# T5 bias of a hybrid decoder layer: read with a positive step from shifted rows instead of reversed on TensorE, and one evacuation of x ahead of a weight split

## The reference, cut to what matters

```
mod = silu(c) @ w_ada + b_ada -> shift1, scale1, gate1, shift2, scale2, gate2
h = rms_norm(x) * (1 + scale1) + shift1                # x is 1024 tokens x 1024
q, k, v, xs, z, B, C, dt = split(h @ w_in)             # one combined projection
a = softmax(q k^T / 8 + bias[head, distance], sinks) v # window 128, 8 heads, blocks of 128
s = Mamba-2 SSD(conv(xs, B, C), dt, A), gated by silu(z)
x = x + gate1 * rms_norm(concat(a, s) @ w_out)
h = rms_norm(x) * (1 + scale2) + shift2
u = causal conv3(h @ w_up);  x = x + gate2 * rms_norm((gelu(u_gate) * u_val) @ w_down)
```

## Time and profile before

| what | value |
|---|---|
| median of 3 runs | 1161.25 us (1160.11 to 1161.86) |
| the profiled execution's own time | 1160.93 us |
| its span, first to last instruction | 1159.0 us |
| PE busy | 1096.3 us, 95% |
| DVE busy | 872.1 us, 75% |
| ACT busy | 548.6 us, 47% |
| POOL (GpSimd) busy | 242.4 us, 21% |
| mean granted TensorE clock | 0.975 |
| DMA moved | 152.71 MB |

### The profile page before, as it was taken

The page is one execution under the profiler, slowest core; times in us unless marked ns, Lnnn a source line. Parts: engine busy times, 40 slices in busy tenths (PEclk is TensorE's granted clock), DMA queues, the critical chain, the costliest instruction groups (busy, mean ns, idle before and its releaser), DMA issues.

```text
span 1159.0 us, 14934 instructions
## 1 busy us (share of the span) xinstructions
PE 1096.3 (95%) x5144; PEld 876.8 (76%) x5144; DVE 872.1 (75%) x1137; ACT 548.6 (47%) x964; POOL 242.4 (21%) x235
## 2 busy tenths in 40 slices
PE   2699999999999999969999999999999999999997
PEld 2578767666777777747888888888888888888885
DVE  5769577767559566587888888888888886776687
ACT  3631255555553343565454444454445455454453
POOL 2100011121212333124333333333333100000012
PEclk7699999999999999989999999999999999999999
DMA  9988311001132101104344343434353496733224
GB/s 342 328 252 300 111 37 37 19 20 37 37 110 91 55 37 55 55 37 146 119 153 139 133 152 119 158 129 158 109 170 109 143 370 220 237 100 98 93 91 164
DMA packets 115359, 152.71 MB, mean 132 GB/s; under 512 B 15148, under 2 KB 75117, under 8 KB 115309
## 3 DMA queue, kind: packets, MB, share of 16 engines
q1 hardware_dynamic: 114989, 151.00, 38.9%
q0 software_dynamic: 320, 1.06, 0.3%
HBM read 121.10 MB, written 30.95 MB: 131 GB/s over the span
## 4 chain that ended last, share of the span: by engine, by line
PE 85%; DVE 6%; ACT 3%; DMA 2%; issue 1%; POOL 1%; SPq 1%; DVEq 0%; POOLq 0%; ACTq 0%
PE ps L2283 34%; PE ps L1938 24%; PE ps L2348 17%; PE ps L1977 2%; PE ps L2003 1%; PE ps L1991 1%; PE ps L2127 1%; DVE big L1255 1%; DMA raw<-in_w_in_dram 1%; ACT big L973 1%; DMA scratch<-in_rel_bias_dram 1%; PE ps L2219 1%; PE ps L2042 1%; DVE a_lo L1524 0%; DVE scratch L1462 0%
## 5 line engine op out<-in xcount | busy, mean ns | idle before, releaser
L1938 PE MATMUL ps<-a_hi,w_hi 128*128 128x512 f32 x416 | 146.1, 429 | 9.0 <-DVE a_lo L1315 6.2
L1938 PE MATMUL ps<-a_lo,w_hi 128*128 128x512 f32 x416 | 132.3, 396 | 0.0
L1938 PE MATMUL ps<-a_hi,w_lo 128*128 128x512 f32 x416 | 131.6, 395 | 0.0
L2348 PE MATMUL ps<-w_hi,a_hi 128*128 128x512 f32 x308 | 119.9, 389 | 0.2 <-DVE a_lo L1771 0.2
L2348 PE MATMUL ps<-w_hi,a_lo 128*128 128x512 f32 x308 | 119.8, 389 | 0.0
L2348 PE MATMUL ps<-w_lo,a_hi 128*128 128x512 f32 x308 | 119.8, 389 | 0.0
L1938 PEld LDWEIGHTS ps<-a_hi,w_hi 128*128 128x128 f32 x416 | 73.6, 192 | 32.6 <-issue 21.9
L1167 ACT ACTIVATE w_hi<-raw 128x512 fp32r<-128x512 f32 x77 | 48.8, 634 | 98.2 <-PE ps L2348 88.4
L1087 ACT ACTIVATE scratch<-ps 128x512 f32<-128x512 f32 x88 | 52.3, 595 | 88.8 <-PE ps L2283 88.7
L1938 PEld LDWEIGHTS ps<-a_hi,w_lo 128*128 128x128 f32 x416 | 78.9, 190 | 18.3
L1938 PEld LDWEIGHTS ps<-a_lo,w_hi 128*128 128x128 f32 x416 | 78.9, 190 | 18.2 <-issue 0.5
(11 more groups left out here) (246 smaller groups left out, 2431.5 us busy)
## 6 DMA issues: line engine op xcount, KB each, us to landing
big<-in_w_ada_dram SPq DMA_DIRECT2D x24, 1024.0 KB, 9.0
raw<-in_w_up_dram SPq DMA_DIRECT2D x22, 512.0 KB, 5.0
big<-in_w_up_dram SPq DMA_DIRECT2D x22, 512.0 KB, 4.6
big<-in_w_down_dram SPq DMA_DIRECT2D x22, 512.0 KB, 6.4
down_weight_sums<-big SPq DMA_DIRECT2D x22, 512.0 KB, 3.4
raw<-down_weight_sums SPq DMA_DIRECT2D x44, 256.0 KB, 2.8
ffn_hidden<-big SPq DMA_DIRECT2D x21, 512.0 KB, 2.6
big<-ffn_hidden SPq DMA_DIRECT2D x21, 512.0 KB, 7.9
```

The source lines that it names most:

```text
L1938: mm = pe.matmul(out, lhs_of[a], rhs_of(b, j), start=first and p == 0, stop=last and p == 2)
L2348: mm = pe.matmul(bk, a[:, ts], rhs_op(s)[w], start=fresh and m == 0, stop=last and m == 2, skip_group_check=s // KH in (J6, J3, J7))
```

## The change

The bias is no longer stored as 8 vectors. One DMA of SyncE (`store_bias_rows`) writes each head's vector 128 times into HBM, into rows that lie 385 elements apart: 1024 rows of 1536 bytes, 1.57 MB, all read from the same 8 partitions of `ext_sb`. Two DMAs (`load_bias_windows`) then read rows of 256 elements with a step of 384 elements for each partition, which gives the rows in their right order, 2 x 512 KB as before. The store stands in SyncE's queue behind `load_late`, the windows behind unit 4's weights and behind a wait for the store. The reversed identity, its load, the four flip matmuls, ACT's four copies and GpSimd's part are gone; the scores wait for the windows themselves. Apart from that, ACT evacuates block 7 of x ahead of `split_hi(0)` instead of behind it.

```diff
     squares = np.concatenate([
-        np.eye(P), i[:, None] <= i[None, :], i[:, None] > i[None, :], np.eye(P)[::-1]], axis=1)
+        np.eye(P), i[:, None] <= i[None, :], i[:, None] > i[None, :]], axis=1)
...
-    bias_d = nc.dram_tensor("bias_by_distance", (H, EXT), f32).ap()
+    bias_d = nc.dram_tensor("bias_rows_shifted", (H, P * (EXT + 1)), f32).ap()
...
-            sp.dma_start(sq[:, :], squares[:, 0:3 * P]).then_inc(s_const, 16)
-            sp.dma_start(flip, squares[:, 3 * P:]).then_inc(s_const, 16)
+            sp.dma_start(sq[:, :], squares).then_inc(s_const, 16)
...
+            def store_bias_rows():
+
+                sp.wait_ge(s_exs, 1)
+                sp.dma_start(bass.AP(bias_d.tensor, 0, [[P * (EXT + 1), H], [EXT + 1, P], [1, EXT]]),
+                             ext_sb.unsqueeze(1).to_broadcast([H, P, EXT])).then_inc(s_bd, 16)
+
+            def load_bias_windows():
+
+                sp.wait_ge(s_bd, 16)
+                for e in range(2):
+                    src = bass.AP(bias_d.tensor, 4 * e * P * (EXT + 1) + P - 1,
+                                  [[EXT, P], [P * (EXT + 1), NPAIR], [1, 2 * P]])
+                    sp.dma_start(bias[:, :, e, :], src).then_inc(s_bw, 16)
...
                     load_late()
+                    store_bias_rows()
+                if n == 4:
+                    load_bias_windows()
...
-            for b in range(2):
+            for b in range(NB):
                 x_rstd(b)
-
-            pool.wait_ge(s_exs, 1)
-            pool.dma_start(bias_d, ext_sb).then_inc(s_bd, 16)
-            for b in range(2, NB):
-                x_rstd(b)
-            pool.wait_ge(s_bd, 16)
-            for e in range(2):
-                src = bass.AP(bias_d.tensor, 4 * e * EXT, [[1, P], [EXT, NPAIR], [1, 2 * P]])
-                pool.dma_start(bias[:, :, e, :], src).then_inc(s_bw, 16)
...
-            act.wait_ge(s_const, 48)
+            act.wait_ge(s_const, 32)
...
+            x_evacuate(NB - 1)
             split_hi(0)
-            x_evacuate(NB - 1)
...
-            for j in range(NPAIR):
-                act.wait_ge(s_flp, j + 1)
-                act.activation(bias[:, j], bank(4 + j).rearrange("p (e k) -> p e k", e=2), ACT.Copy)\
-                    .then_inc(s_bias, 1)
...
+                if u == 0:
+                    dve.wait_ge(s_bw, 32)
...
-                    if n == 1 and k == 2:
-                        bias_flip()
...
-                    pe.wait_ge(s_bias, NPAIR)
```

More of the change, by code:

```diff
@@ L139, in hybrid_layer_kernel @@
         ident, upper, strict = sq[:, 0:P], sq[:, P:2 * P], sq[:, 2 * P:3 * P]
-        flip = scratch[:, 3840:3968]
         raw_dt = scratch[:, 3968:4032].rearrange("p (k h) -> p k h", k=KT)
@@ L346, in hybrid_layer_kernel @@
         s_wm = [sem(f"middle_w_out_loaded{i}") for i in range(2)]
-        s_bd, s_bw = sem("bias_vectors_stored"), sem("bias_windows_loaded")
+        s_bd, s_bw = sem("bias_rows_stored"), sem("bias_windows_loaded")
         s_xr = [sem(f"x_reloaded{i}") for i in range(2)]
@@ L364, in hybrid_layer_kernel @@
         s_ext, s_exs = sem("bias_vectors_in_psum"), sem("bias_vectors_ready")
-        s_flp, s_bias = sem("bias_flipped"), sem("bias_ready")
         s_dtT, s_dtn = sem("dt_evacuated"), sem("dt_transposed")
@@ L1883, in _ @@
         def _(pe):
-            pe.wait_ge(s_const, 48)
+            pe.wait_ge(s_const, 32)
             def x_transpose(b):
@@ L2006, in values @@
                 mm.then_inc(s_pv, 1)
[L2008 to L2013, removed]
             def v_transpose():
```

## The result

The changed kernel takes 1185.12 us (median of 4 runs, 1183.22 to 1187.69) where the kernel before took 1161.55 (4 runs, 1160.11 to 1162.09): ratio 1.0206, 95% interval 1.0184 to 1.0228, 23.6 us slower. The profiled execution took 1183.22 us with a span of 1181.1 and a mean granted clock of 0.978.

The account below looks back on a forecast made before the run. PE, 95% busy, was taken to bound the kernel, with 1.8 us of slack at chunk 9. Store delay +25.3 and clock +0.5 gave +25.8 on 1160.93, 1186.7, plus 0.32 for the median: 1187.0 us, range 1162 to 1192.

Parts of the forecast that it names:

- Part 1: Head: the load of the reversed identity, which ACT's first instruction waited for, is gone; 0.2 us off (0 to 0.5).
- Part 2: Head: ACT evacuates block 7 before its split, so DVE's modulate starts at about 45.85 instead of 47.53; 1.7 us off.
- Part 3: PE's chain: the flip's eight matmuls, 3.43 us, are gone, but the store swallows the gain.
- Part 4: SyncE's queue: the store from 8 partitions takes 29 us ahead of chunk 6 and unit 3's weights; +25.3 us.
- waits for chunk 9 once more: One-column matmuls: PE, with 23.5 us of work against DVE's 25.9, waits for chunk 9's sum and starts at 139.4.
- the formula: Time change at unit 3's weights and chunk 9: store - 1.9 - 1.8, here +25.3 us; a free store gives only 3.7.
- Part 5: PE after its 28 us wait: clock falls to 1.2 GHz, slow matmuls cost some 3 us against 2.4 slack; +0.5 us.
- Part 6: SyncE's queue behind unit 4's weights: the windows' 1 MB, 2.5 us, falls into the idle stretch; no cost.
- Rival 1: The store is bound by eight engines, not its partitions: 7.5 to 12 us, total 1165 to 1170; chance 0.17.
- Rival 2: The store runs at nearly full rate over all 16 engines: 3.7 to 6 us, total 1161 to 1163.5; chance 0.08.
- Rival 3: The store delays nobody, its transfers fitting beside the loads: 3.7 to 5.3 us off, 1156 to 1157.5; chance 0.12.

Follow-up runs that it names:

- t1: Kernel before with one edit: block 7 of x evacuated ahead of the first split; 1159.5 us, ratio 0.9981.
- t2: Kernel before without the flip and ACT's four copies, the bias used with its rows reversed; 1159.3 us, ratio 0.9983.
- t3: Kernel before with both edits of t1 and t2, bias rows again reversed, no store of rows; 1155.49 us, ratio 0.9951.
- s2: Changed kernel with the store's eight source rows in partitions 0, 4, ..., 28 instead of 0 to 7; 1164.92 us, ratio 1.0036.
- u1: Changed kernel with a second, equal store into another HBM tensor, the windows waiting for both; 1218.07 us, ratio 1.0495.
- u4: s4 with stored rows 512 elements (2048 bytes) apart; 1156.28 us, ratio 0.9955.
- s4: s3 with the store issued ahead of SyncE's wait for h's last low part and of load_late; 1157.07 us, ratio 0.9963.
- s1: Changed kernel with stored rows 512 elements apart instead of 385, windows read with a step of 511; 1185.03 us, ratio 1.0214.
- s3: Changed kernel storing from all 128 partitions, each head's vector held in 16 and each stored 8 times; 1164.2 us, ratio 1.0030.
- u2: Changed kernel with its 8-partition store put ahead of the wait for h's last low part and of load_late; 1182.41 us, ratio 1.0186.
- u3: s3 with stored rows 512 elements (2048 bytes) apart; 1160.68 us, ratio 0.9995.

## Why the prediction was right

The time, 1185.1 where 1187.0 was forecast, and the side are right, and so is the step that carries them.

**Part 1, the head (-0.2).** Not seen. DVE's modulation columns came at 45.85 (45.61 before), and PE's first unit starts between 48.2 and 52.7 us over the thirteen profiled kernels, much more than 0.2.

**Part 2, block 7 ahead (-1.7).** Right: t1 gave 1.9. Modulate started at 46.05, right behind the columns, as forecast for 45.8; PE's first unit at 50.01 against 49.6. What the prediction only noted in passing, that w_in's load has no windows beside it any more, goes with a split that waits 0.30 instead of 3.99 us; t1, where the windows stayed, still waits 3.10. What that alone is worth wasn't measured.

**Part 3, the flip (-3.43).** Right that the eight matmuls go, and that the store swallows this. Without a store t2 keeps 2.1 us of it and t3 gains 5.9 where block 7 alone gains 1.9.

**Part 4, the store (29 us).** Right in mechanism and size: 50 to 52 GB/s at half of the engines (share 0.46 to 0.47) where it runs alone, over about 72 to 102 us. At unit 3's weights it is worth 27.4 us. The step from the rows' 33 us down to 29 had no row behind it, so that it hit so closely is partly luck; 33 would have given 1191. Low part's end: 112.04 against 113.4 forecast; PE's wait: 27.15 against 28; one-column matmuls: 137.20 against 139.4. DVE's chain kept its 25.9 us: chunk 9's sum ended at 137.96. That its source's partitions set the price, s2 shows; that nothing of a longer store is hidden, u1.

The step that was wrong is where PE is held, "waits for chunk 9 once more", with the slack of 1.8 us there. PE started the one-column matmuls 0.76 us before chunk 9 was summed and lost nothing (3.63 us as before); starting 1.85 and 1.88 us early cost it 0.51 (t3) and 1.06 (t2). In the changed kernel their start follows from unit 3's low part alone: 112.04, plus the 23.5 us of PE's work, plus 1.6 us of low clock in unit 3, is 137.1. The next hold is at the gate sums within unit 6, by chunk 11, and the slack there was 1.74 us before. But that too is no fixed number. In the kernel before the clock fell behind the one-column matmuls, in the changed one it didn't. One window of each:

```profile
118.00:122.00 4.00, 4.00 (x12) 3.11 (x11) 3.86 (x6) 0.76 (x1) 0.00 (x0) 0.57 1.08 352
```
```profile
141.00:145.00 4.00, 4.00 (x19) 3.27 (x18) 2.13 (x3) 1.98 (x2) 0.00 (x0) 1.00 1.03 358
```

From unit 5's start to the gate sums PE took 15.32 us before (117.35 to 132.67) and 15.24 after (140.69 to 155.93), of which 1.33 were the wait for chunk 11: 1.41 us less work. Without the low clock the slack of before would thus have been 0.3 us. That 1.8 and 1.74 are nearly equal is chance, so the formula came out right for the slow stores by luck in this term. It was too cautious where no store delays DVE: 3.7 us forecast as the most a free store could give, 5.9 measured in t3 and 5.7 in u4.

**Part 5, the clock (+0.5).** The drop came: 0.50 in the window of 94 to 102 us. Unit 3 took 12.47 us instead of 10.9 (112.09 to 124.56), so its slow matmuls cost 1.6 us, not 3. That is under the 2.4 us of slack that the forecast set against them, and the +0.5 didn't come. It and the store's 27.4 instead of 29 are the 2 us by which the forecast was high. A second effect wasn't foreseen. The long block took 393.57 us before and 392.28 after. A window of the kernel before at the block's start, then one of the changed kernel:

```profile
547.00:553.00 6.00, 5.62 (x18) 4.50 (x19) 5.45 (x4) 4.00 (x6) 3.42 (x2) 0.72 0.23 93
```
```profile
570.00:577.00 7.00, 6.25 (x27) 5.17 (x28) 6.45 (x5) 5.19 (x8) 3.46 (x2) 1.00 0.25 102
```

The clock column says 0.72 and 1.00. The block took 393.6 us in the profiles of before, t1, t2, s2, s4 and u1, and 392.3 in those of the changed kernel, t3, s1, s3, u2, u3 and u4, which cuts across every edit. In the profiles these 1.3 us belong to what the changed kernel falls short of the forecast and to what t3 gained beyond 3.7. What decides it is open.

**Part 6, the windows (0).** Right: they are issued at 108.96 us, and DVE's first use of the bias, at 170.69, starts without a wait.

**The rivals.** Rival 1, eight engines and 1165 to 1170, is near what s2 shows once the rows are spread: 1164.92. Rival 2's near full rate needs both the 128 partitions and rows 2048 bytes apart (u3, 1160.68). Rival 3, a store that delays nobody and 1156 to 1157.5, is u4 at 1156.28: it took the early issue as well, so the idle stretch of 60 to 66 us was worth something, but only to a store that is short.

## What to carry to other kernels

This store, which read eight neighbouring partitions, was priced by those partitions and not by its bytes, and the weights behind it in the queue paid nearly all of it: ask first which partitions a DMA touches, then what is queued behind. Here making the same rows from 128 partitions, 2048 bytes apart and issued where the engines are idle, turned +23.6 us into -5.7. And a slack read at one wait is worth checking at the waits before and behind it, and against the clock in the stretch: PE was not held at the one that looked tightest.

## What the runs showed of the hardware that was not expected

- Rows of 1536 bytes stored 1540 bytes apart moved at 186 to 234 GB/s with all engines busy, and 2048 bytes apart at 387 to 401 GB/s (s3, u3). Read from partitions 0 to 7, the pitch made no difference (50 and 53 GB/s).
- Half of the engines moved 200 GB/s from eight partitions that lie four apart (s2, share 0.57) and 50 GB/s from eight neighbouring ones (share 0.46).
- A slow store in the queue holds the issuing engine too: SyncE needed 17.93 and 17.70 us to issue chunk 6 and unit 3's weights, against 2.97 and 4.87 before.
- A second equal store delayed unit 3 by 33.9 us more, where the first delayed it by 27.4 (u1, by distance).
